# Running sums of the log forget gates: fp32 products replaced by products in the short format, a rounded part and the rest

## The chip, the cores and the metric

The kernel runs on one core of a Trainium2 chip. The metric is the device time of one execution in microseconds (us), lower is better; three timed runs are given for the kernel before, and one further execution was profiled. The core's engines work side by side and meet through semaphores: PE (matrix products; PEld is its loading of the stationary operand), DVE (vector), ACT (activations), POOL (GpSimd) and SP, which here only issues DMAs.

## The reference

A sequence of 256 tokens of width 1024 goes through two blocks. The first has two layers (l = 0, 1), each an RMS norm, a hybrid mixer with three kinds of attention heads (A sparse, B chunk band, C "forgetting"), gates, and a SwiGLU feed-forward. The second block has a MoBA layer and a dilated layer, each with a squared-ReLU feed-forward. The change touches the five C heads of the two layers of the first block:

```python
log_f = jax.nn.log_sigmoid(f_logit.astype(jnp.float32))
F = jnp.moveaxis(jnp.cumsum(log_f, axis=1), 1, 2)
...
logits = (jnp.einsum('bqhd,bshd->bhqs', qs, k).astype(jnp.float32) * scale
          + Fq[..., :, None] - F[:, :, None, :])
```

`F` is the running sum over the 256 tokens of the log of the forget gate, one row for each head; every logit of the head gets the sum at its query minus the sum at its key.

## The kernel before

**Format.** All data is fp32. The large products are made in a short format (`F32R`), in which a number is kept as a rounded part ("hi") and, in a second tile, the rest ("lo"); each product then is hi x hi, lo x hi and hi x lo, three products in place of one. For every unit of weights (two tiles of 128 x 512) a DMA issued by SP fills `raw_units`, ACT rounds it to `hi_units` (L1371), POOL subtracts to get `lo_units` (L733), and PE uses both (L789, L832, L834, L835). Small products, transposes, scores and the sums over the gates are made in plain fp32.

**Tokens.** The 256 tokens are two tiles of 128. P = 128, S = 256, HC = 5 C heads, NT = 2 token tiles.

**Order around the change.** The attention of a layer runs in steps k = 0, 1, 2, ..., one head scored in each, written out by hand on every engine and in order on each. In each step PE transposes (L1013) or scores (L997, L1000) and then works one unit of the gate weights (12 products at L789), so weight products are woven between the heads. In steps 3 to 8 `forget_products` comes in between:

- Step 3 (c = 0): three small products (L1270 to L1272) with the triangular constant `tri` as stationary operand and `LF`, 128 tokens x 5 heads for each token tile, as moving one. They give the running sums with tokens on partitions, and DVE copies them to `F8` (L2188).
- Steps 4 to 8 (c = 1 to 5), one C head each: the head's column of `LF`, broadcast to 128 columns, is the stationary operand, and `tri` is the moving one, 256 columns for the first token tile (L1276) and 256 for the second (L1277). The result is the running sum along the free axis on all 128 partitions of `BANK[TP]`. DVE makes the head's mask of it (`forget_masks`, L2192 and L2193).

`LF` comes from DVE and ACT in the steps before: DVE takes -z and its minimum with z (L2148, L2149, event "nabs"), ACT an exponential (L1715), DVE four small operations (L2154 to L2157), ACT a logarithm (L1718), DVE two more (L2160, L2161, event "logf"), all on 128 x 10 elements. Scratch of this chain (`ZN`, `ZE`, `ZD`) lies in PSUM.

**tri.** It is a 128 x 384 constant: 8 where 128 + p <= column, else 0. Its columns 0 to 127 are all zero, 128 to 255 are the triangle, 256 to 383 are all 8. It lies in the tile `constants`, filled by a DMA.

**POOL.** Beside the `lo_units`, POOL makes eight modulation sums in the first layer (L698, L702), one after every fourth unit from the first gate unit on.

## Time and profile before

| | |
|---|---|
| timed runs | 1460.19, 1459.61, 1456.82 us; median 1459.61 us |
| profiled execution, its own time | 1456.65 us |
| its span (first to last instruction) | 1454.8 us |
| granted TensorE clock, mean | 0.997 |
| PE matrix products | 1432.1 us busy, 98% |
| POOL | 1210.1 us busy, 83% |
| ACT / DVE | 52% / 50% |

The profile lists, for one execution, what each engine did and what released it when it had waited. "Busy" of PE is modelled at its ends, so two products in a row overlap in the records: the duration of one record is more than the time that it takes of the engine. What a product takes of the engine is read from the chain of work that ended last, which divides the time among the instructions one after another. An fp32 product shows as two loads and two matrix records (x2 for one instruction).

### The profile page before, as it was taken

The numbers are of one execution on the slowest core, as the hardware profiler recorded it, in microseconds if no ns is written. First come the engines' busy times: TensorE is split into PE (matmuls) and PEld (weight loads), VectorE is DVE, ScalarE is ACT, GpSimd is POOL, SyncE is SP. The second block draws the span as 40 slices with busy tenths as digits, with TensorE's granted clock in tenths as the row PEclk, the third lists the DMA queues.
The fourth block names the chain that finished last, engine by engine and source line by source line (L and its number), as shares of the span: only waits on it lengthen the run. The fifth ranks groups of instructions, "written<-read, shape, count | busy, mean of one in ns | idle before, by whom it ended". The sixth has DMA issues, their size and how long they took to land.

```text
span 1454.8 us, 21549 instructions
## 1 busy us (share of the span) xinstructions
PE 1432.1 (98%) x7600; PEld 1199.7 (82%) x7600; DVE 723.9 (50%) x1557; ACT 755.6 (52%) x1272; POOL 1210.1 (83%) x984
## 2 busy tenths in 40 slices
PE   7999999999999999999999999999999999999997
PEld 5898777799988987778888888778888888788886
DVE  7863654766643754745566304454650044655202
ACT  4435774644444445765544445674654346655431
POOL 3899989888878986559898997966999977789994
PEclk9999999999999999999999999999999999999999
DMA  9994547689875996337676565644566755456651
GB/s 362 402 354 159 199 168 225 230 292 327 313 265 168 401 319 200 117 99 232 219 242 201 187 204 169 191 142 145 189 195 197 222 162 181 131 164 198 199 197 52
DMA packets 149415, 313.35 MB, mean 215 GB/s; under 512 B 10918, under 2 KB 31802, under 8 KB 149307
## 3 DMA queue, kind: packets, MB, share of 16 engines
q1 hardware_dynamic: 147552, 310.62, 63.8%
q10 hardware_dynamic: 1756, 1.35, 0.3%
q8 instruction: 61, 1.00, 0.3%
q14 instruction: 46, 0.38, 0.1%
HBM read 310.87 MB, written 1.06 MB: 214 GB/s over the span
## 4 chain that ended last, share of the span: by engine, by line
PE 92%; DVE 4%; ACT 1%; POOL 1%; DMA 1%; issue 1%; SPq 0%; DVEq 0%; ACTq 0%
PE bank L789 58%; PE bank L834 12%; PE bank L835 8%; PE bank L832 5%; PE bank L997 1%; PE bank L981 1%; POOL lo_units L733 1%; PE bank L870 1%; PE bank L967 1%; DMA x_rows<-in_x 1%; PE bank L1078 1%; PE bank L1013 1%; PE bank L1049 1%; PE bank L1039 0%; PE bank L1092 0%
## 5 line engine op out<-in xcount | busy, mean ns | idle before, releaser
L733 POOL TENSOR_TENSOR lo_units<-raw_units,hi_units 128x512 fp32r<-128x512 f32 (+3 forms) x928 | 1151.4, 1276 | 221.7 <-ACT hi_units L1371 220.6
L1371 ACT ACTIVATE hi_units<-raw_units 128x1024 fp32r<-128x1024 f32 (+1 forms) x470 | 482.6, 1030 | 411.1 <-PE bank L789 251.9
L789 PE MATMUL bank<-hi_units,turned 128*128 128x512 f32 (+3 forms) x1600 | 441.2, 390 | 1.2 <-DVE turned L1897 0.7
L789 PEld LDWEIGHTS bank<-hi_units,turned 128*128 128x128 f32 x1600 | 291.7, 189 | 53.5 <-issue 3.3
L835 PE MATMUL bank<-turned,lo_units 128*128 128x256 f32 x1024 | 288.0, 281 | 0.0
L789 PE MATMUL bank<-hi_units,turned_wide 128*128 128x512 f32 x992 | 274.5, 391 | 0.0
L834 PE MATMUL bank<-turned,hi_units 128*128 128x512 f32 x736 | 259.2, 397 | 0.0
L789 PE MATMUL bank<-lo_units,turned 128*128 128x512 f32 (+3 forms) x800 | 252.8, 383 | 0.9 <-POOL lo_units L733 0.5
L789 PEld LDWEIGHTS bank<-hi_units,turned_wide 128*128 128x128 f32 x992 | 185.3, 188 | 38.4 <-issue 0.5
L835 PEld LDWEIGHTS bank<-turned,lo_units 128*128 128x128 f32 x1024 | 194.4, 190 | 0.2
L789 PEld LDWEIGHTS bank<-lo_units,turned 128*128 128x128 f32 x800 | 149.7, 188 | 30.6 <-POOL lo_units L733 3.7
L834 PEld LDWEIGHTS bank<-turned,hi_units 128*128 128x128 f32 x736 | 138.1, 188 | 33.1
L789 PE MATMUL bank<-lo_units,turned_wide 128*128 128x512 f32 x496 | 160.8, 390 | 0.0
L1849 DVE SCALAR_TENSOR_TENSOR bank<-ada_units,small,bank 128x512 f32<-128x512 f32 x148 | 111.9, 756 | 31.8 <-DMA ada_units<-in_ada_w 27.0
L789 PEld LDWEIGHTS bank<-lo_units,turned_wide 128*128 128x128 f32 x496 | 93.1, 188 | 20.0 <-POOL lo_units L733 0.4
L1915 DVE TENSOR_REDUCE bank<-bank 128x256 f32<-128x512 f32 x92 | 64.4, 700 | 85.2 <-PE bank L835 84.4
L832 PE MATMUL bank<-turned,hi_units 128*128 128x256 f32 x576 | 104.0, 283 | 0.0
L832 PEld LDWEIGHTS bank<-turned,hi_units 128*128 128x128 f32 x576 | 90.2, 192 | 0.6
L1781 ACT ACTIVATE mlp_relu<-bank 128x256 f32<-128x256 f32 x56 | 21.5, 384 | 59.2 <-DVE bank L1915 58.7
L2321 DVE SCALAR_TENSOR_TENSOR bank<-x_rows,bank 128x512 f32<-128x512 f32 x8 | 5.2, 692 | 87.0 <-PE bank L789 87.0
L1911 DVE TENSOR_TENSOR turned_wide<-bank,turned_wide 128x256 fp32r<-128x256 f32 x92 | 39.0, 424 | 15.9 <-ACT turned_wide L1421 13.2
L2334 DVE SCALAR_TENSOR_TENSOR bank<-x_rows,bank 128x512 f32<-128x512 f32 x8 | 5.6, 696 | 75.8 <-PE bank L789 75.6
(261 smaller groups left out, 1288.6 us busy)
## 6 DMA issues: line engine op xcount, KB each, us to landing
ada_units<-in_ada_w SPq DMA_DIRECT2D x88, 512.0 KB, 7.8
raw_units<-in_w_ffn_tiles SPq DMA_DIRECT2D x72, 512.0 KB, 5.2
raw_units<-in_mlp_w_out SPq DMA_DIRECT2D x64, 512.0 KB, 3.3
raw_units<-in_mlp_w_tiles SPq DMA_DIRECT2D x56, 512.0 KB, 3.2
raw_units<-in_w_in SPq DMA_DIRECT2D x56, 458.0 KB, 9.7
raw_units<-in_w_in SPq DMA_DIRECT2D x48, 512.0 KB, 6.9
raw_units<-in_w_ffn_out SPq DMA_DIRECT2D x44, 512.0 KB, 3.5
raw_units<-in_moba_w_qkv SPq DMA_DIRECT2D x24, 512.0 KB, 3.7
```

Of the source, the lines that this page charges most:

```text
L733: pool.tensor_tensor(LO[:, s, b, 0:w], RAW[:, u["slot"], b, 0:w], HI_[:, s, b, 0:w].bitcast(F32), ALU.subtract).then_inc(lo_ready.sem, lo_ ...
L789: ins = pe.matmul(BANK[2 * c["pair"] + t][:, 0:w], (A[a] if A is BT else A[:, a])[:, part, t * P:(t + 1) * P], W[:, s, b, 0:w], start=(i = ...
L832: pe.matmul(bank[:, 0:S], HI_[:, s, b, at:at + P], A[:, kt, part, :], start=kt == 0 and part == 0, stop=False)
L834: pe.matmul(bank[:, :], HI_[:, s, b, at:at + P], A[:, kt, :, :].rearrange("p two s -> p (two s)"), start=kt == 0, stop=False)
L835: ins = pe.matmul(bank[:, 0:S], LO[:, s, b, at:at + P], A[:, kt, 0, :], start=False, stop=kt == KT - 1)
L870: ins = pe.transpose(BANK[(TQ, TP)[n % 2]][:, j * P:(j + 1) * P], src[:, t, (4 * half + j) * P:(4 * half + j + 1) * P], con("ident"))
L967: pe.matmul(bank[n * DH:(n + 1) * DH, 0:S], src[:, 0, values[n]:values[n] + DH], turned_probs[n][:, 0:S], start=True, stop=False)
L1371: act.activation(HI_[:, s, 0:n, 0:w], RAW[:, u["slot"], 0:n, 0:w], ACT.Copy)\
L1781: act.activation(RTN[:, m % 4, :], BANK[(TQ, TP)[m % 2]][:, 0:S], ACT.Relu).then_inc(act_side.sem, act_side.mark(("relu tile", i, m)))
L1849: ins = v.scalar_tensor_tensor(total, raw[:, k, :], COND[:, kt:kt + 1], partial, ALU.mult, ALU.add)
L1911: tell(v.tensor_tensor(AT[:, n, 1, :], h, AT[:, n, 0, :].bitcast(F32), ALU.subtract), turned_lo, (tag, "tile", n))
L1915: return v.tensor_reduce(to, bank[:, :].rearrange("p (two s) -> p s two", two=2), AX_X, ALU.add)
```

## The change

The products of steps 4 to 8 are made in the short format. DVE writes, once, a rounded copy of the 256 columns of `tri` that are not zero over the constant itself (8 and 0 are the same in the short format). In each layer DVE writes `LF` in two parts into the new tile `forget_rounded`: this turns one operation into four (L2161 before). Each head's two fp32 products become four: rounded part and rest of the first token tile's column against 256 columns of `tri`, and rounded part and rest of the second token tile's against the 128 columns in which the product is not zero. The three products of step 3 stay in fp32, their operand read through a view of the same memory. The new tile is placed after `ones_rounded`, so that the tiles behind it (`raw_units`, `hi_units`, `lo_units` and most others) move up by its 80 bytes, rounded up to 96.

```diff
     ONES = ONES_R[:, :].bitcast(F32)
+    LFR, _ = place("forget_rounded", [P, 2, NT * HC], F32R)
     RAW, _ = place("raw_units", [P, NR, UNIT_K, CW])
...
-    CON, _ = place("constants", [P, n_const])
+    CON, con_at = place("constants", [P, n_const])
+    CON_R, _ = place("constants_rounded", [P, n_const], F32R, at=con_at)
+    TRI_R = CON_R[:, cat["tri"][0] + P:cat["tri"][1]]
+    TRI = TRI_R.bitcast(F32)
...
-                    pe.matmul(BANK[TP][:, 0:HC], con("tri")[:, P:2 * P], lf[:, 0, :], start=True, stop=True)
-                    pe.matmul(BANK[TP][:, HC:2 * HC], con("tri")[:, S:3 * P], lf[:, 0, :], start=True, stop=False)
-                    pe.matmul(BANK[TP][:, HC:2 * HC], con("tri")[:, P:S], lf[:, 1, :], start=False, stop=True)\
+                    pe.matmul(BANK[TP][:, 0:HC], TRI[:, 0:P], lf[:, 0, :], start=True, stop=True)
+                    pe.matmul(BANK[TP][:, HC:2 * HC], TRI[:, P:S], lf[:, 0, :], start=True, stop=False)
+                    pe.matmul(BANK[TP][:, HC:2 * HC], TRI[:, 0:P], lf[:, 1, :], start=False, stop=True)\
                         .then_inc(forget.sem, forget.mark((l, "cols")))
                     return
                 pe.wait_ge(rows.sem, rows.at(("forget cols", l) if c == 1 else ("forget mask", l, c - 2)))
-                pe.matmul(BANK[TP][:, 0:S], LF[:, c - 1:c].to_broadcast([P, P]), con("tri")[:, P:3 * P], start=True, stop=False)
-                pe.matmul(BANK[TP][:, 0:S], LF[:, HC + c - 1:HC + c].to_broadcast([P, P]), con("tri")[:, 0:S], start=False, stop=True)\
-                    .then_inc(forget.sem, forget.mark((l, c - 1)))
+                for t, cols, onto in ((0, slice(0, S), slice(0, S)), (1, slice(0, P), slice(P, S))):
+                    for part in range(2):
+                        ins = pe.matmul(BANK[TP][:, onto], LFR[:, part, t * HC + c - 1:t * HC + c].to_broadcast([P, P]), TRI_R[:, cols],
+                                        start=(t, part) == (0, 0), stop=(t, part) == (1, 1))
+                ins.then_inc(forget.sem, forget.mark((l, c - 1)))
...
             dve.wait_ge(late_const_in, 16)
+            if l == 0:
+                v.tensor_copy(TRI_R, con("tri")[:, P:3 * P])
             z = PROJ[:, :, FC:FC + HC]
...
                     link(v.tensor_tensor(ZL, ZL, ZD, ALU.subtract))
-                    say(v.scalar_tensor_tensor(LF, ZN, 0.0, ZL, ALU.max, ALU.add), ("logf", l))
+                    link(v.scalar_tensor_tensor(ZN, ZN, 0.0, ZL, ALU.max, ALU.add))
+                    v.tensor_copy(LF, ZN)
+                    link(v.tensor_copy(LFR[:, 0, :], ZN))
+                    say(v.tensor_tensor(LFR[:, 1, :], ZN, LFR[:, 0, :].bitcast(F32), ALU.subtract), ("logf", l))
```

`link` makes the next DVE operation wait for this one; `say` raises the event that others wait for.

## Rows read from the trace of the kernel before

**Rows 1.** The page: busy time and share by engine, and the chain by engine.
```profile
PE 1432.1 (98%) x7600; PEld 1199.7 (82%) x7600; DVE 723.9 (50%) x1557; ACT 755.6 (52%) x1272; POOL 1210.1 (83%) x984
...
PE 92%; DVE 4%; ACT 1%; POOL 1%; DMA 1%; issue 1%; SPq 0%; DVEq 0%; ACTq 0%
```

**Rows 2.** Busy time by stretch: us, then each engine, PE clock, DMA share, GB/s.
```profile
125.00:150.00 25.00, 25.00 (x130) 20.10 (x126) 10.59 (x27) 12.42 (x18) 24.31 (x20) 1.00 0.47 154
...
555.00:580.00 25.00, 25.00 (x126) 20.15 (x128) 10.92 (x27) 12.42 (x18) 15.82 (x13) 1.00 0.55 168
```

**Rows 3.** The chain in order of time, 100 to 160 us: start, us, what.
```profile
121.65 0.22 PE bank L1013 x2
...
125.78 0.22 PE bank L1271 x2
...
129.34 0.43 PE bank L1276 x2
129.77 0.43 PE bank L1277 x2
130.21 2.74 PE bank L789 x12
...
133.80 0.63 PE bank L1276 x2
134.43 0.43 PE bank L1277 x2
```

**Rows 4.** Lines L1276 and L1277: min/median/max ns, and who waited (us, times).
```profile
L1276 PEld LDWEIGHTS bank<-constants,small x20: 185/188/193, 129.1 to 575.8; 128*128 128x128 f32 x20
L1276 PE MATMUL bank<-constants,small x20: 379/380/483, 129.2 to 576.1; 128*128 128x256 f32 x20
...
  DVE forget_masks L2192: 25.6, 10
```

**Rows 5.** The chain in order of time, 390 to 430 us, feed-forward of layer 0.
```profile
390.00 0.12 PE bank L835
390.12 0.24 PE bank L832 x2
```

**Rows 6.** The page: one of the costliest groups, loads of a short-format operand.
```profile
L835 PEld LDWEIGHTS bank<-turned,lo_units 128*128 128x128 f32 x1024 | 194.4, 190 | 0.2
```

**Rows 7.** Timeline, 209 to 229 us: start, us, engine, line; [idle before <-releaser].
```profile
209.09 5.02 POOL L733 TENSOR_TENSOR lo_units<-raw_units,hi_units 128x512 fp32r<-128x512 f32 x4
...
217.35 0.38 ACT L1490 ACTIVATE turned<-bank 128x256 fp32r<-128x256 f32 x1 [3.29 <-PE bank L969]
...
218.76 2.54 POOL L733 TENSOR_TENSOR lo_units<-raw_units,hi_units 128x512 fp32r<-128x512 f32 x2 [4.65 <-ACT hi_units L1371]
...
228.67 0.30 PEld L789 LDWEIGHTS bank<-lo_units,mixed_turned 128*128 128x128 f32 x2 [0.30 <-POOL lo_units L733]
```

**Rows 8.** Timeline, 116 to 126 us, the chain that makes LF in layer 0.
```profile
116.56 0.17 DVE L2149 TENSOR_TENSOR small<-bank,proj_rows 128x10 f32<-128x10 f32 x1
...
117.16 0.18 ACT L1715 ACTIVATE bank<-small 128x10 f32<-128x10 f32 x1
...
121.00 0.17 DVE L2161 SCALAR_TENSOR_TENSOR small<-bank,small 128x10 f32<-128x10 f32 x1
...
122.80 0.74 DVE L2029 SCALAR_TENSOR_TENSOR idx_scores<-bank,proj_rows,idx_scores 128x256 f32<-128x256 f32 x2 [1.63 <-ACT bank L1526]
...
125.40 0.39 PE L1270 MATMUL bank<-small,constants 128*128 128x5 f32 x2
```

**Rows 9.** Groups of DVE by shape, 90 to 130 us: busy us, mean ns | idle before.
```profile
L1854 DVE CAST mod_rounded<-bank 128x512 fp32r<-128x512 f32 x1 | 0.7, 691 | 0.0
...
L2133 DVE TENSOR_TENSOR proj_rows<-bank,row_vectors 128x326 f32<-128x326 f32 x2 | 1.0, 488 | 0.0
...
L2133 DVE TENSOR_TENSOR proj_rows<-bank,row_vectors 128x52 f32<-128x52 f32 x2 | 0.4, 202 | 0.0
```

## The prediction, made before the changed kernel ran

> **What bounds the kernel now.** I read the page first: busy shares, then the chain that ended last [rows 1]. PE is busy 98% of the span, and 92% of the chain is PE's. An average can hide a stage with another limit, so the second view is the busy time by stretch over the steps that the change touches: 125 to 150 us in layer 0 and 555 to 580 us in layer 1 [rows 2]. PE is busy in all 25 us of both, at a granted clock of 1.00 (the 2.4 GHz level). DVE and ACT are below half. POOL is not: 24.31 of 25 us in layer 0, 15.82 in layer 1, so in layer 0 a second engine is nearly full, and whether it lets a gain through has to be shown. The third view is the chain in order of time [rows 3]. There PE's instructions follow one another without a foreign piece, and each has its true share of the engine's time. A microsecond less of PE work in these steps is then a microsecond less of the chain, unless something later holds it up.
>
> **The products of one head, before.** The fp32 product of 256 columns takes 0.43 us, the first and the second token tile's alike [rows 3]: 0.86 us a head. In half of the steps the first stands with 0.63 us: there the products of the scores, which use 64 rows, come ahead of it in place of a transpose, and the 0.20 us more is a price of the changeover (a weight product in that place pays about the same), so it stays. The records of one instruction are two, with 188 ns for the load and 380 ns for the product [rows 4]; they overlap, and the 0.43 us is two passes of about 0.216 us. Line L1276 has 20 records, so 10 products: 5 heads in 2 layers, and 10 heads pay 8.6 us in all.
>
> **The products of one head, after.** Two short-format products have 256 columns. The feed-forward of layer 0 has just these: 0.12 us each, 0.24 us for two [rows 5]. That is 256 columns at 2.4 GHz, 0.107 us, and 0.013 us on top. So the first token tile costs 0.24 us.
>
> The second tile's two products have 128 columns, and no short-format product of the trace has so few. Two rows bound them. From below: PE needs a load before each product, and the loads alone set a pace. The small fp32 products of 5 columns take 0.22 us for two passes, 0.11 us a load, and two transposes of 128 columns take 0.22 us, again 0.11 us each [rows 3]. The load's record is as long in the short format (190 ns) as in fp32 (188 ns) [rows 4, 6], so I see no faster load. From above: the fp32 rate, where 256 columns cost 0.43 us, so 128 cost 0.215 us, in case the short format has its speed only at the widths at which this kernel has used it. I take 0.11 us, since the transpose has the same width and the load the same length, and since 256 columns in short format (0.12 us) already are so near the load's pace that a narrower product should meet it. Both ends go into the range.
>
> Sum for a head: 0.24 + 2 x 0.11 = 0.46 us, in place of 0.86 to 0.87 (the chain's 0.43 pieces begin 0.43 and 0.44 us apart, so 0.865). Saved: 0.405 us a head, **4.05 us** for ten. At the upper bound: 0.24 + 0.43 = 0.67, saved 0.195, 1.95 us for ten.
>
> The Trainium skill ("TensorE: Matmul & The Clock Gate", back-to-back issue gap) gives an isolated gap of N/2.4 plus 2.5 ns, 56 ns for 128 columns, and speaks of loads that run during the product before. By that page the two narrow products would cost 0.11 us together and the saving would be about 5 us; the same page's load time, 128 columns at 1.2 GHz or 107 ns, agrees with the 0.11 us of rows 3. It is weighed as a rival below.
>
> **DVE's added work.** In layer 0 one copy of 128 x 256 comes ahead of "nabs". A cast of 128 x 512 took 0.69 us [rows 9], so it costs between 0.2 (the shortest DVE operations) and 0.36 us (half of the cast); I take 0.35. It moves the end of L2149 from 116.73 to about 117.1 us. ACT begins its exponential at 117.16 [rows 8], right behind its own table load, which ended about then: the copy is covered, by less than 0.1 us. Without cover it would cost nothing on PE either, because of the next slack. At "logf" the one operation (0.17 us) is followed by three more, about 0.2 us each with the link: 0.6 us, in each layer. L2161 ends at 121.17 us, and PE comes to L1270 at 125.40 [rows 8]: 4.2 us of slack, 3.6 after the change, 3.2 if the copy's 0.35 us went through. Behind it on DVE waits L2029, at 122.80 after 1.63 us idle, so that 0.6 us fits in too. Layer 1 has the same order and no copy. All of it: 0. If the cover were gone, at most 0.35 + 0.6 + 0.6, about 1.6 us.
>
> **DVE's masks.** L2192 waited 25.6 us over ten heads for L1277 [rows 4]; it will start 0.4 us sooner, and PE does not wait for it. Step 3 keeps its instructions. No DMA is added or moved.
>
> **Does POOL let layer 0's gain through?** From the attention's start POOL works nearly without a pause. But it stops: at 209.09 it does four operations, until 214.11, and is then idle for 4.65 us until ACT's `hi_units`; ACT in turn, in order, had waited 3.29 us for PE's L969 until 217.35 [rows 7]. So at 218.76 POOL is late because PE is, not for its own work. If PE arrives 2.0 us earlier (five heads), so do ACT and POOL, and POOL's pause shrinks to about 2.6 us. After it the one wait of PE for POOL, 0.30 us at 228.67 [rows 7], keeps its size and moves along. I let the whole gain through.
>
> **The sum.** Against the profiled execution: span 1454.8 - 4.05 = 1450.7 us, its own time 1456.65 - 4.05 = 1452.6. That execution lies 3.0 us below the median of the three timed runs, which themselves span 3.4 us. Against the median: 1459.61 - 4.05 = **1455.5 us**, 0.28% less. About 0.3% (4.4 us) is what a measurement of this kernel can tell from no change, so the forecast falls just inside "same".
>
> **Rivals.**
>
> *Narrow short-format products run at the fp32 rate.* For it: nowhere does the kernel use the short format below 256 columns, so no row shows its speed there. Against: nothing in 256, 458 or 512 columns hints at a step. Time 1459.6 - 1.95 = 1457.7 us.
>
> *Narrow products are bound by streaming, not by the load.* For it: loads overlap products in the records. They would cost 0.053 + 0.013 = 0.067 us each; a head 0.37, saved 0.49, in all 4.9 us: 1454.7 us, 0.34% less. Against: transposes and 5-column products at 0.11 us. The Trainium skill's gap (same page) is this rival with another constant.
>
> *Layer 0's gain is lost to POOL.* For it: POOL at 97% in the steps, PE's 0.30 us wait at 228.67. Against: the 4.65 us pause. It decides once PE is ahead by more than the pause. If all of layer 0 were lost, 2.0 us are left: 1457.6 us; with narrow products at the fp32 rate, 1.0 us: 1458.6 us.
>
> *Slower: the 96-byte move of the tiles.* Nearly all big tiles start at another address. If POOL's subtraction (2.51 us for a unit, two of its five-microsecond four) were slower at the new address, it would reach PE's 2.74 us a unit [rows 3, 7] at 9% more. From there every per cent costs 0.025 us on some 460 units, 11.5 us; one per cent over the point would end at about 1467 us. Against: DVE's additions at L2133 start at columns of all sorts, yet 52 and 326 columns took 202 and 488 ns [rows 9], 1.04 ns a column, with other widths on the same line: engines don't mind the address there.
>
> **Chances.** Forecast (load-bound) 0.42; fp32 rate 0.32; streaming-bound 0.08; layer 0 lost, wholly or partly 0.10; slower by the move or by something unforeseen 0.08. Range: from the streaming case, 1454.7, less half the spread of the runs (1.7), 1453.0, to the lost case with the fp32 rate, 1458.6, plus 1.2 for the spread of a median, 1459.8. It leaves out the slower case and little else. Faster by over 0.3% (below 1455.2): forecast 0.42 x 0.4, streaming 0.08 x 0.8, fp32 rate 0.32 x 0.05: 0.25. Slower: 0.08. Same: 0.67.
>
> **What would show it.** In the chain of the changed kernel each head's four products should take 0.12, 0.12, 0.11 and 0.11 us; 0.21 in the last two is the fp32 rate, 0.07 is streaming. They should have one record each, not two, with loads of about 188 ns. The small operations before "logf" should end near 121.8 us with PE's L1270 unmoved at 125.4. POOL's pause near 218 us should be about 2.6 us and PE's wait at 228 us still 0.3. The step from 129 to 147 us in layer 0 should be 2.0 us shorter, and every later landmark earlier by the same amount up to layer 1, then by 4.0. The prediction is wrong if the products cost more than 0.86 us a head, if PE waits for `lo_units` or `hi_units` where it did not, or if POOL's 1.25 us an operation has changed.

## The result, and the profile after

The change made the kernel slower by 0.3%: 1462.95 us, the median of 7 runs (1460.90 to 1464.31), against 1459.13 us for the kernel before in 7 runs beside them; ratio 1.0029, 95% interval 1.0018 to 1.0041. The forecast was 1455.5 us, and its range (1453.0 to 1459.8) does not hold the result. The profiled execution has a span of 1462.1 us, 7.3 more than before's. That is more than the medians' 3.8 us, since before's profiled execution lies 2.5 us below its median and the changed kernel's 1.0 above: what is read from this pair of traces is exact for the two executions and larger than the loss of a typical one.

The page of the changed kernel, busy time and chain, answers to [rows 1]:

```profile
PE 1431.4 (98%) x7600; PEld 1194.6 (82%) x7600; DVE 724.0 (50%) x1564; ACT 755.6 (52%) x1272; POOL 1209.6 (83%) x984
...
PE 70%; DMA 11%; POOL 9%; DVE 6%; ACT 3%; issue 1%; SPq 1%; DVEq 0%; ACTq 0%; POOLq 0%
...
L737 POOL TENSOR_TENSOR lo_units<-raw_units,hi_units 128x512 fp32r<-128x512 f32 (+3 forms) x928 | 1150.8, 1276 | 229.5 <-ACT hi_units L1377 227.9
```

The busy times are those of before, POOL's 1276 ns for one operation too. What changed is who holds the chain: DMA 11% and POOL 9%, in place of 1% each. (Lines behind the new code stand four to eleven further down: L793 is the old L789, L1001 the old L997, L1377 the old L1371, L1282 the new products.) PE's waits, us in total, times, longest:

```profile
PE bank L1001 <- DVE idx_scores L2035: 4.0, 1, 4.0
PE bank L793 <- ACT hi_units L1377: 2.6, 3, 1.1
PE bank L1001 <- ACT qk_turned L1521: 1.4, 1, 1.4
```

Before had one wait of 0.5 us for `hi_units`, ahead of the changed steps, and neither of the other two. The busy table of the steps answers to [rows 2]; layer 0's stretch has 4 us less of PE, with 136 GB/s moved in it:

```profile
125.00:150.00 25.00, 20.99 (x107) 16.80 (x104) 8.14 (x21) 10.46 (x15) 24.31 (x19) 0.93 0.43 136
555.00:580.00 25.00, 25.00 (x137) 19.91 (x138) 10.36 (x32) 16.18 (x24) 21.49 (x18) 1.00 0.79 256
```

The granted clock of layer 0's stretch is 0.93 too, where before had 1.00. That is taken up after the wait.

The chain through the 4.0 us wait, in order of time (answers to [rows 3]):

```profile
132.55 6.48 DMA raw_units<-in_w_in
...
139.05 0.03 ACT hi_units L1377
...
140.13 1.28 ACT L1715
...
141.43 1.06 ACT gate_rows L1715
142.48 0.27 ACT qk_turned L1521
...
143.27 0.75 DVE idx_scores L2035 x2
...
144.15 0.70 PE bank L1001 x4
...
146.05 4.04 PE bank L793 x12
```

DVE is named as the releaser, but it only passes on a delay that came with a transfer. Raw units landed at 139.03 us; ACT works in order, so the table load, the gates and the scores' inputs queued behind its `hi_units`. The timelines of ACT, first before, then after:

```profile
135.12 1.06 ACT L1371 ACTIVATE hi_units<-raw_units 128x1024 fp32r<-128x1024 f32 x1 [0.81 <-DMA raw_units<-in_w_in]
```

```profile
139.05 1.06 ACT L1377 ACTIVATE hi_units<-raw_units 128x1024 fp32r<-128x1024 f32 x1 [5.34 <-DMA raw_units<-in_w_in]
```

ACT was already waiting 0.81 us for this transfer before, and now the transfer lands 3.9 us later. PE still had about 0.9 us of slack behind it: DVE ended its part at 140.3 us, and PE came to those scores at 141.36. After the change DVE ends 3.7 us later and PE comes 1.2 us sooner (140.14 us); less the slack, that makes the 4.0 us.

Of the 3.9 us only 1.7 are the transfer's own time (6.48 us in place of 4.82). For 2.3 us it was issued later, and it was issued later because POOL, which frees the raw units, was later. First the issue by SP, before and after (two issues to a row), then POOL, before and after:

```profile
130.28 0.98 SPq L675 DMA_DIRECT2D raw_units<-in_w_in  x2
```

```profile
132.55 1.80 SPq L679 DMA_DIRECT2D raw_units<-in_w_in  x2
```

```profile
83.95 25.24 POOL L733 TENSOR_TENSOR lo_units<-raw_units,hi_units 128x458 fp32r<-128x458 f32 x22
```

```profile
91.62 7.03 POOL L737 TENSOR_TENSOR lo_units<-raw_units,hi_units 128x458 fp32r<-128x458 f32 x6 [0.82 <-ACT hi_units L1377]
98.89 6.81 POOL L737 TENSOR_TENSOR lo_units<-raw_units,hi_units 128x456 fp32r<-128x456 f32 x6 [0.25 <-ACT hi_units L1377]
106.67 4.81 POOL L737 TENSOR_TENSOR lo_units<-raw_units,hi_units 128x456 fp32r<-128x456 f32 x4 [0.97 <-ACT hi_units L1377]
```

Before, POOL worked from 84 to 109 us without a pause. Now it ran out of input three times, 2.0 us in all, and each time ACT's rounding ahead of it had waited for a transfer. From 106.67 us to beyond 180 us POOL is full in both kernels, so it stays 2.3 us late and the transfers that wait for it with it.

The wait has a second price. Right behind it the granted clock fell to the 1.2 GHz level, from 145.1 to 148.5 us: the mean of this stretch is 0.52 (1.00 before), PE's products stand 427 ns apart, and one unit takes 4.04 us in place of 2.74. Against the products-alone kernel below, without this wait, PE lost 1.6 us there:

```profile
145.00:148.50 3.50, 3.50 (x12) 2.93 (x11) 1.48 (x4) 1.44 (x2) 3.24 (x4) 0.52 0.00 0
```

And the transfers themselves are slower. Busy by stretch, in a stretch where the DMA engines are full (last two numbers: DMA share, GB/s), before, then after:

```profile
18.00:44.00 26.00, 23.86 (x125) 19.11 (x124) 21.16 (x34) 12.11 (x18) 14.22 (x12) 0.93 1.05 403
```

```profile
18.00:44.00 26.00, 23.94 (x125) 19.09 (x124) 20.32 (x34) 12.22 (x18) 13.38 (x12) 0.93 1.05 368
```

The DMA share is the same 1.05, the bytes are 9% fewer. The change adds no transfer. It moves where they land: `raw_units` from byte 38528 to 38624 of each partition, the tiles of the adaLN rows from 122496 and 151808 to 122592 and 151904. (From `mod_rows` on the tiles move by 128 bytes, since that tile is placed on the next multiple of 64.)

To compare kernels, the rest of this text divides the time between two landmarks, the start of PE's instruction 500 (at 115.8 us, ahead of all changed products) and its last one, into PE's waits and the time without them, called pace. Before: 1330.4 us, 5.1 of it waits. All such figures are of one execution a kernel.

| kernel | total, us more | waits | products | other pace |
|---|---|---|---|---|
| the change | +7.65 | +7.9 | -4.0 | +3.8 |

The -4.0 is measured below; the last column is what is left, and the fallen clock is 1.6 us of it. So the products gave what was forecast, and the move of the tiles took more, in three ways: waits for late transfers, the clock behind the longest of them, and a PE that runs slower without waiting. In this pair of traces it took nearly three times as much (11.7 us), by the medians of the next section 6.8 us.

### The profile page after: what moved, and what is told of

Read it like the earlier page. It is cut to its first block, busy times and chain, and to the rows that moved or that the text cites. A ratio compares the mean times of both kernels' runs of the same rounds, so it can differ in the third digit from the quotient of the medians.

```text
span 1462.1 us, 21556 instructions
## 1 busy us (share of the span) xinstructions
PE 1431.4 (98%) x7600; PEld 1194.6 (82%) x7600; DVE 724.0 (50%) x1564; ACT 755.6 (52%) x1272; POOL 1209.6 (83%) x984
## 3 DMA queue, kind: packets, MB, share of 16 engines
q10 hardware_dynamic: 1756, 1.35, 0.3%
## 4 chain that ended last, share of the span: by engine, by line
PE 70%; DMA 11%; POOL 9%; DVE 6%; ACT 3%; issue 1%; SPq 1%; DVEq 0%; ACTq 0%; POOLq 0%
PE bank L793 44%; PE bank L838 12%; POOL lo_units L737 8%; PE bank L839 6%; DMA raw_units<-in_w_in 4%; DMA raw_units<-in_w_ffn_tiles 3%; DMA ada_units<-in_ada_w 2%; ACT hi_units L1377 1%; DVE bank L1855 1%; DMA raw_units<-in_w_ffn_out 1%; PE bank L1001 1%; PE bank L985 1%; PE bank L874 1%; PE bank L971 1%; DMA x_rows<-in_x 1%
## 5 line engine op out<-in xcount | busy, mean ns | idle before, releaser
L737 POOL TENSOR_TENSOR lo_units<-raw_units,hi_units 128x512 fp32r<-128x512 f32 (+3 forms) x928 | 1150.8, 1276 | 229.5 <-ACT hi_units L1377 227.9
L1377 ACT ACTIVATE hi_units<-raw_units 128x1024 fp32r<-128x1024 f32 (+1 forms) x470 | 482.9, 1031 | 422.3 <-PE bank L793 210.0
L793 PE MATMUL bank<-hi_units,turned 128*128 128x512 f32 (+3 forms) x1600 | 444.2, 392 | 2.3 <-ACT hi_units L1377 1.7
L793 PEld LDWEIGHTS bank<-hi_units,turned 128*128 128x128 f32 x1600 | 291.4, 189 | 58.0 <-issue 3.3
L793 PE MATMUL bank<-hi_units,turned_wide 128*128 128x512 f32 x992 | 274.7, 391 | 0.9 <-ACT hi_units L1377 0.9
L793 PE MATMUL bank<-lo_units,turned 128*128 128x512 f32 (+3 forms) x800 | 255.2, 386 | 1.0 <-POOL lo_units L737 0.6
L838 PE MATMUL bank<-turned,hi_units 128*128 128x512 f32 x736 | 255.8, 392 | 0.0
L793 PEld LDWEIGHTS bank<-hi_units,turned_wide 128*128 128x128 f32 x992 | 185.2, 188 | 39.8 <-issue 1.8
L793 PEld LDWEIGHTS bank<-lo_units,turned 128*128 128x128 f32 x800 | 149.8, 188 | 33.0 <-POOL lo_units L737 4.3
L793 PE MATMUL bank<-lo_units,turned_wide 128*128 128x512 f32 x496 | 161.0, 390 | 0.6 <-POOL lo_units L737 0.5
L793 PEld LDWEIGHTS bank<-lo_units,turned_wide 128*128 128x128 f32 x496 | 93.0, 188 | 21.3 <-POOL lo_units L737 1.9
```

Of the source, the lines that this page charges most:

```text
L737: pool.tensor_tensor(LO[:, s, b, 0:w], RAW[:, u["slot"], b, 0:w], HI_[:, s, b, 0:w].bitcast(F32), ALU.subtract).then_inc(lo_ready.sem, lo_ ...
L793: ins = pe.matmul(BANK[2 * c["pair"] + t][:, 0:w], (A[a] if A is BT else A[:, a])[:, part, t * P:(t + 1) * P], W[:, s, b, 0:w], start=(i = ...
L838: pe.matmul(bank[:, :], HI_[:, s, b, at:at + P], A[:, kt, :, :].rearrange("p two s -> p (two s)"), start=kt == 0, stop=False)
L1377: act.activation(HI_[:, s, 0:n, 0:w], RAW[:, u["slot"], 0:n, 0:w], ACT.Copy)\
```

## The experiments

**Move and products apart.** The first kernel is the one before with a gap of 96 bytes; the second is the change with `forget_rounded` placed last, so that no tile moves.

```diff
     ONES = ONES_R[:, :].bitcast(F32)
+    plan_at[0] += 96
     RAW, _ = place("raw_units", [P, NR, UNIT_K, CW])
```

> The kernel before, with nothing changed but an empty gap of 96 bytes ahead of raw_units, so that raw_units, hi_units, lo_units and the tiles behind move as they do in the changed kernel. Theory A (the move slows the DMAs: from 17 us on each 512 KB transfer of the changed kernel landed 1.36 us after the one before it, against 1.25 before): transfers of the first 100 us at about 1.36 us, the attention of layer 0 stalls PE for some 4 us near 144 us, and the time is 1459 + 4 (what the products save, now missing) + 3.8 = about 1466 to 1468 us, ratio 1.005 or more. Theory B (the added DVE work or the order of the products made the stalls, the slower DMAs are chance): 1.25 us a transfer, no stall at 144 us, ratio 1.000.

```diff
-    LFR, _ = place("forget_rounded", [P, 2, NT * HC], F32R)
     RAW, _ = place("raw_units", [P, NR, UNIT_K, CW])
...
     POS, _ = place("positions_int", [P, NT], I32)
+    LFR, _ = place("forget_rounded", [P, 2, NT * HC], F32R)
```

> The changed kernel, with forget_rounded placed behind the last tile, so that every tile of the kernel before stays at its address. Theory A: no stall near 144 us, transfers at 1.25 us, four products of a head at 0.41 us, ratio 0.997 (1459.1 - 4.4 = 1454.7 us). Theory B: the stall of 4 us stays, ratio 1.003.

The gap alone: 1465.90 us, ratio 1.0045 (1.0033 to 1.0057). The products alone: 1455.48 us, ratio 0.9979 (0.9970 to 0.9987). That this is the forecast to 0.02 us is luck: by its ratio it is 3.1 us less than before, by the medians of that round (1459.12 before) 3.6, and 4.05 were forecast. The same stretch as above, of the gap and then of the products:

```profile
18.00:44.00 26.00, 25.68 (x118) 20.72 (x117) 20.45 (x33) 10.89 (x17) 12.91 (x11) 0.93 1.05 368
```

```profile
18.00:44.00 26.00, 25.91 (x119) 20.91 (x118) 20.44 (x33) 11.07 (x17) 12.66 (x11) 0.93 1.05 403
```

The gap alone slows the transfers as the change did. Its wait near 144 us was 1.1 us, not the 4 that I expected, and its clock did not fall there: PE comes to the same late data at 142.7 us in place of 140.1, about half of it by its longer products and half because instruction 500 started 1.3 us later in this execution. From instruction 500 to 700 the second kernel gains 2.0 us, over layer 1's heads (3000 to 3300) 2.0 again: 4.0 us, with `LFR` and all else of the change in place. It doesn't keep all of it. A wait of PE at 180.6 us grew from 0.27 to 0.82 us, and the chain leads back from there over DVE, ACT and a transfer to POOL, which holds 11% of this kernel's chain.

**Other distances of the move.** The change with 32 more bytes behind `forget_rounded` (all moves by 128) or 160 more (by 256), and the kernel before with a gap of 64 or 32.

```diff
     LFR, _ = place("forget_rounded", [P, 2, NT * HC], F32R)
+    plan_at[0] += 32     # after128; 160: after256
```

> The changed kernel, with 32 bytes of padding behind forget_rounded, so that the tiles move by 128 bytes in place of 96. If it is the address within 64 bytes (theory A1), transfers at 1.25 us and ratio 0.997, as without a move. If any move from the addresses of the kernel before slows (A2, neighbours or wider alignment), 1.36 us and 1.003. Theory B: 1.003.

> The changed kernel with 160 bytes of padding behind forget_rounded, so that the tiles move by 256 bytes and lie in the 256-byte windows as in the kernel before. Theory G: as with forget_rounded placed last: ada_units 1.25 us and raw_units 1.18 us a transfer, ratio 0.998, 1455.5 us. If it is the distance moved or the neighbours in memory that counts: 1458 us or more, as with 128 bytes.

```diff
+    plan_at[0] += 64     # hole64; 32: hole32
     RAW, _ = place("raw_units", [P, NR, UNIT_K, CW])
```

> The kernel before with an empty gap of 64 bytes ahead of raw_units. A1 (64 bytes are the grain): 1.25 us a transfer, ratio 1.000. If the grain is 128 bytes (A3): slower transfers, ratio 1.005. Theory B: ratio 1.000.

> The kernel before with an empty gap of 32 bytes ahead of raw_units. Theory G (a row of a transfer costs by the number of 256-byte windows of the destination that it touches): raw_units then starts 160 bytes into a window, its rows of 1832 bytes (160 + 1832 = 1992) touch 8 windows as before (128 + 1832 = 1960), and go at about 77 ns a packet; rows of 2048 bytes touch 9 unless they start on a window. So it behaves like the gap of 64 bytes: transfers of raw_units at 1.2 us, of ada_units at 1.36, ratio 1.000 to 1.002. Theory H (a start that is no multiple of 64 bytes is slow): as the gap of 96 bytes: 88 ns a packet, 1.34 us, ratio 1.0045.

Measured: moved by 128, 1458.65 us, ratio 1.0007 (0.9990 to 1.0023); its profiled execution took 1465.32 us, far above that median, so its waits are not used here. Moved by 256, 1456.45, ratio 0.9981 (0.9963 to 0.9999): the gain is back. Gap of 64, 1459.59, 1.0006 (0.9993 to 1.0019). Gap of 32, 1464.28, 1.0042 (1.0028 to 1.0057). The last is a miss that points ahead: its packets of 1832 bytes took 78 ns, as the window theory has it, and yet it is as slow as the 96-byte gap.

The time between two landings in a full stretch, from the traces, gives the rule. A unit of full rows (2048 bytes each) into the adaLN tiles takes 1.25 to 1.27 us where the tile starts on a multiple of 256 and 1.35 to 1.36 us where it doesn't; the packets of 1832 bytes into `raw_units` take 76 to 78 ns each (median) with the tile at 0, 128, 160 or 192 modulo 256, and 88 ns at 224 (the change and the 96-byte gap). Counted in windows of 256 bytes, 2048 bytes touch 8 on a multiple and 9 elsewhere; 1832 bytes touch 8 from any of the first four places and 9 from 224. The Trainium skill ("DMA: Bandwidth & Descriptors", section "How a descriptor splits into AXI transactions") gives the split into 256-byte transactions as the vendor's account, and words its rule for an unaligned start as one of reading; these rows show the like on the side that is written, in the core's memory. A ninth window is 12.5% more; 8% (1.35 against 1.25 us) and 14% (1.34 against 1.18 us for a raw unit) were measured.

**All bulk destinations on multiples of 256.** The products-alone kernel, and the kernel before, with the plan's start, `gate_rows`, `mod_rows` and `scores` rounded up.

```diff
-    plan_at = [-(-nc.sbuf_base // 64) * 64]
+    plan_at = [-(-nc.sbuf_base // 256) * 256]
...
     PROJ, union = place("proj_rows", [P, NT, PROJ_W])
+    plan_at[0] = -(-plan_at[0] // 256) * 256
...
-    MOD, mod_at = place("mod_rows", [P, 6 * D], at=-(-one_end // 64) * 64)
+    MOD, mod_at = place("mod_rows", [P, 6 * D], at=-(-one_end // 256) * 256)
```

> The changed kernel with forget_rounded last and every tile that a DMA fills starting on a multiple of 256 bytes (all tiles 128 bytes up, gate_rows and mod_rows padded to the next multiple). Theory G: the last transfers of 9 windows a row go too: the first units of ada_units from 1.35 to 1.25 us each, and raw_units with 2048-byte rows. PE waits for these only in the first 60 us, so 0.5 to 2 us less than with forget_rounded last alone: 1453.5 to 1455 us, ratio 0.996 to 0.9975. Without G: no difference from 0.998.

> The kernel before with all tiles that a DMA fills on multiples of 256 bytes, as in the aligned changed kernel. If placement and products add up: 1458.95 - (1455.5 - 1452.0) = 1455.5 us, ratio 0.9977, and the aligned changed kernel is 4 us below it. If the alignment only paid together with shorter products: ratio 1.000.

With the change's products 1451.99 us, ratio 0.9956 (0.9940 to 0.9971), the fastest kernel of all; without them 1455.19, ratio 0.9981 (0.9966 to 0.9997). Difference 3.2 us (by the two ratios 3.6): products and placement add up. But the full stretch is not faster than before's 403:

```profile
18.00:44.00 26.00, 24.32 (x123) 19.80 (x122) 20.23 (x32) 11.06 (x16) 13.50 (x12) 0.93 1.05 402
```

**Which products pay.** The products-alone kernel with the second token tile on 256 columns, as the first; and the kernel before, still fp32, with only the second token tile narrowed to 128.

```diff
-                for t, cols, onto in ((0, slice(0, S), slice(0, S)), (1, slice(0, P), slice(P, S))):
+                for t, cols in ((0, slice(P, 3 * P)), (1, slice(0, S))):
```

> forget_rounded last, and the second token tile's two products on 256 columns, the first 128 against the zeros of tri, as in the kernel before (the rounded copy is made of 384 columns). It measures what the narrow products save. Load-bound narrow products (0.11 us): 0.02 us a head, ratio as with narrow ones, 0.998. Streaming-bound (0.06 us, as their starts in the trace of the changed kernel lie apart): 0.12 us a head, 1.2 us in all, ratio 0.9987.

```diff
-                pe.matmul(BANK[TP][:, 0:S], LF[:, HC + c - 1:HC + c].to_broadcast([P, P]), con("tri")[:, 0:S], start=False, stop=True)\
+                pe.matmul(BANK[TP][:, P:S], LF[:, HC + c - 1:HC + c].to_broadcast([P, P]), con("tri")[:, P:S], start=False, stop=True)\
```

> The kernel before with one edit: the fp32 product of the second token tile on its 128 columns that are not zero. It needs no rounding, no tile and no DVE work. 128 columns at the fp32 pace are 0.215 us, so 0.215 us a head are saved, 2.15 us in all: 1456.8 us, ratio 0.9985. If a narrow fp32 product were held to the wide one's time: 1.000.

The full width takes 1455.95 us, ratio 0.9978 (0.9963 to 0.9992), no different from 1455.48. The fp32 kernel takes 1456.86, ratio 0.9985 (0.9968 to 1.0003), which as a time is not clear of no change; between the landmarks its two groups of heads take 1.0 us less each. A head in the chain, in order of time, narrow short format (products alone), full short format, narrow fp32:

```profile
558.89 0.40 PE bank L1282 x4
559.29 2.81 PE bank L793 x12
```

```profile
558.56 0.47 PE bank L1283 x4
559.02 2.75 PE bank L794 x12
```

```profile
129.63 0.43 PE bank L1276 x2
130.06 0.22 PE bank L1277 x2
130.28 2.73 PE bank L789 x12
```

The narrow products save 0.07 us, and the weight products behind them take 0.06 to 0.07 us longer: 3.21 and 3.22 us. In the short format the narrowing is worth nothing; in fp32 it halves the second product.

**Transfers or something else?** Two kernels split the gap: 96 bytes ahead of `raw_units` with 160 more ahead of `proj_rows`, and 64 bytes ahead of `proj_rows` alone.

```diff
+    plan_at[0] += 96     # rawonly
     RAW, _ = place("raw_units", [P, NR, UNIT_K, CW])
...
+    plan_at[0] += 160    # rawonly; 64 here and nothing above: adaonly
     PROJ, union = place("proj_rows", [P, NT, PROJ_W])
```

> The kernel before with a gap of 96 bytes ahead of raw_units and one of 160 ahead of proj_rows: raw_units, hi_units, lo_units and row_vectors lie as in the changed kernel, the tiles behind as in the kernel before within their 256-byte windows. Transfers of raw_units at 88 ns a packet and 1.33 us, of ada_units at 1.25. If the windows of raw_units make the loss of the changed kernel: stalls of PE near 144 or 420 us and ratio 1.003 or more. If it is those of ada_units: ratio 1.000.

> The kernel before with a gap of 64 bytes ahead of proj_rows: raw_units, hi_units and lo_units stay, ada_units loses its place on a multiple of 256. Transfers of raw_units at 76 ns a packet and 1.18 us, of ada_units at 1.35 us. As with the gap of 64 bytes ahead of raw_units: ratio 1.000 to 1.001 if ada_units alone costs nothing. If it carries the loss: 1.003.

They took 1466.65 us (1.0053, 1.0033 to 1.0073) and 1464.99 us (1.0044, 1.0028 to 1.0059). These are the slow branches of both expectations, but without the stalls that were to make them: between the landmarks their waits are 0.2 and 0.3 us shorter than before's. All of the loss, 9.9 and 6.3 us, is pace. The theory that only late transfers cost time falls. In the last 90 us PE does nothing but 512-column products on `hi_units` or `lo_units` and `turned_wide`; the busy table there, before, then the 64-byte kernel:

```profile
1380.00:1440.00 60.00, 60.00 (x266) 49.67 (x266) 2.59 (x4) 21.29 (x21) 53.21 (x42) 1.00 0.42 140
```

```profile
1380.00:1440.00 60.00, 60.00 (x259) 48.32 (x258) 2.59 (x4) 22.51 (x22) 54.79 (x44) 1.00 0.49 158
```

259 products in place of 266 in 60 us, at a granted clock of 1.00 and with no wait. The transfers there are far from full (0.49). Sorted by operands, these products start 233 ns apart in place of 227, while those on `turned` keep their 227; in the kernels with one gap it is the other way round. What `turned_wide` and `turned` share is the second operand, so the next theory was the distance between the two operands, modulo 256 bytes, which is 0 for both pairs before.

**Operand distance alone.** Three edits of the kernel before, each with 256 bytes in two parts, so that at most one thing changes modulo 256: `turned` (distance), `hi_units` with `lo_units` (distance to both), `raw_units` (a destination, no distance).

```diff
+    plan_at[0] += 96     # turned96
     HT, turned_at = place("turned", [P, KT, 2, S], F32R)
...
+    plan_at[0] += 160    # turned96; 96: raw96
     RAW, _ = place("raw_units", [P, NR, UNIT_K, CW])
+    plan_at[0] += 96     # hi96; 160: raw96
     HI_, _ = place("hi_units", [P, NH, UNIT_K, CW], F32R)
     LO, _ = place("lo_units", [P, NH, UNIT_K, CW], F32R)
+    plan_at[0] += 160    # hi96
     VEC, _ = place("row_vectors", [P, NV, CW])
```

> The kernel before with only turned (and the small tiles behind it) moved by 96 bytes, all others by 256: DMA destinations keep their place modulo 256, the distance from turned to hi_units changes by 160 modulo 256. Distance theory: products on hi_units and turned start 231 ns apart in place of 227, those on turned_wide stay at 227; feed-forward of layer 0 a little faster; no new waits; DMA 403 GB/s; in all 2 to 4 us more: about 1462 us. Rival (PE's pace follows the slower transfers): pace and time as before, 1459 us.

> The kernel before with 96 bytes between raw_units and hi_units and 160 behind lo_units: no bulk DMA destination changes modulo 256, hi_units and lo_units move against both turned and turned_wide. Distance theory: products on turned and on turned_wide both start 231 to 233 ns apart, as in the run that moved the raw units by 96 and the rest by 256; DMA 403 GB/s, no new waits; 7 to 10 us more: 1466 to 1469 us. Rival (slower transfers set PE's pace): 1459 us.

> The kernel before with 96 bytes ahead of raw_units and 160 behind it, so that only raw_units stand at another place modulo 256 (224 in place of 128). Window theory for the transfers: rows of 1832 bytes touch 9 windows of 256 in place of 8, DMA falls to about 384 GB/s in 18 to 44 us. Distance theory: PE's pace is untouched (227 ns with either operand). What is left are waits for late raw units, near none where only raw units are slow: 1459 to 1461 us. Rival (the earlier run's 7.5 us came from the raw units' place): 1466 us.

All three came out as the distance theory has it in the main: 1462.78 us (1.0029, 1.0014 to 1.0044), 1468.06 us (1.0065, 1.0043 to 1.0088) and 1457.79 us (0.9993, 0.9980 to 1.0006). The first missed in its details: products on `turned` start 234 ns apart and not 231, and layer 0's feed-forward was not faster (107.5 us, before 107.4). The full stretch of the second and third:

```profile
18.00:44.00 26.00, 24.32 (x123) 19.81 (x122) 20.20 (x32) 11.07 (x17) 13.50 (x12) 0.93 1.05 403
```

```profile
18.00:44.00 26.00, 25.32 (x118) 19.91 (x117) 20.38 (x32) 10.54 (x16) 11.99 (x11) 0.80 1.05 386
```

The slowest kernel of all has transfers as fast as before's; the one with slower transfers loses nothing that can be measured. The last 90 us, of `turned96` and of `hi96`:

```profile
1380.00:1440.00 60.00, 60.00 (x266) 49.69 (x265) 2.59 (x4) 23.32 (x22) 56.12 (x45) 1.00 0.51 167
```

```profile
1380.00:1440.00 60.00, 60.00 (x259) 48.27 (x258) 2.59 (x4) 23.08 (x22) 54.46 (x44) 1.00 0.50 166
```

Only the kernel in which `turned_wide`'s distance changed is slow here.

**Can distance be used for a gain?** In the kernel with the 64-byte gap layer 0's feed-forward (256-column products on `turned`) ran faster, 114 ns a product in place of 120. The aligned kernel with `turned` moved by 64, or by 192, and the rest by 256:

```diff
+    plan_at[0] += 64     # turned64; 192: turned192
     HT, turned_at = place("turned", [P, KT, 2, S], F32R)
...
+    plan_at[0] += 192    # turned64; 64: turned192
     RAW, _ = place("raw_units", [P, NR, UNIT_K, CW])
```

> The aligned kernel with the tile turned moved by 64 bytes and everything behind it by 256, so that only the distance from turned to hi_units and lo_units is changed against 256-byte multiples (it was whole) and every tile that DMA fills in bulk stays on a multiple of 256. Distance theory (PE's pace depends on how far apart its two operands lie, modulo 256 bytes): the 768 products of 256 columns in layer 0's feed-forward start 114 ns apart in place of 120, 4.2 us less; the 512-column products with turned gain or lose under 1 us; time 1452.0 - 4.2 = 1447.8 us, DMA at 402 GB/s in 18 to 44 us. Rival (the pace in the 64-byte kernel came from slower DMA writes, not from the distance): 1452.0 us and 120 ns.

> The aligned kernel with turned moved by 192 bytes and everything behind it by 256, so that hi_units lie 64 bytes further from turned, modulo 256, as in the kernel of before with a 64-byte gap (the run that moved turned by 64 had them 64 bytes nearer, the other sign, and its feed-forward products started 118 ns apart). Distance theory with its sign: layer 0's feed-forward products on turned and hi_units start 114 ns apart (120 when the distance is whole), 4.2 us less in 304 to 404 us; the products of 512 columns with turned 2 ns more at the median, those with turned_wide 227; the 64-byte run's pace without its waits was 1.5 us ahead of before from 116 us on, which gives 1452.0 - 1.5 = 1450.5 us. Rival (that pace belonged to the places of other tiles, or to the slower transfers, in the 64-byte run): 118 or 120 ns, 1452 us or more.

1460.13 us (1.0021, 1.0005 to 1.0037) and 1456.23 us (0.9986, 0.9977 to 0.9996); both missed their times. The 256-column products start 118 ns apart in the first and 116 in the mean in the second, where the 864 of them in layer 0 took 103.8 us in place of 107.4. With the same distance of 64 the gap kernel had 113 at the median, so the distance alone does not set this number. And the second kernel's other stretches were 5.9 us slower than the aligned kernel's, and its waits 1.2 us longer. My sum had taken the 64-byte kernel's 1.5 us off the aligned kernel, whose pace was already 2.4 us ahead of before. The aligned kernel with whole distances stays the best.

The parts between the two landmarks against before, in us (the pace of kernels with the change's products has their -4.0 in it), and the median time between the starts of two products that follow each other on these operands, in ns. The columns of 512 are the products that stream the weights (L789), the last one is layer 0's feed-forward:

| kernel | hi_units minus turned, mod 256 | hi_units minus turned_wide | waits | pace | 512 columns, turned | 512, turned_wide | 256, turned |
|---|---|---|---|---|---|---|---|
| before | 0 | 0 | 0 | 0 | 227 | 227 | 120 |
| products alone | 0 | 0 | +1.0 | -2.8 | 227 | 227 | 120 |
| the change, moved by 256 | 0 | 0 | +0.6 | -5.3 | 228 | 227 | 120 |
| aligned | 0 | 0 | +0.8 | -6.4 | 228 | 227 | 120 |
| before, aligned | 0 | 0 | +0.3 | -2.3 | 227 | 227 | 120 |
| the change | 96 | 0 | +7.9 | -0.2 | 232 | 227 | 117 |
| the change, moved by 128 | 128 | 0 | +2.1 | +0.5 | 232 | 227 | 119 |
| gap 96 | 96 | 0 | +3.8 | +2.9 | 232 | 227 | 117 |
| gap 64 | 64 | 0 | +4.3 | -1.5 | 229 | 227 | 113 |
| aligned, turned by 64 | 192 | 0 | +0.6 | +1.2 | 233 | 227 | 118 |
| aligned, turned by 192 | 64 | 0 | +2.0 | -4.2 | 229 | 227 | 117 |
| gap 32 | 32 | 0 | +0.8 | +6.0 | 234 | 227 | 117 |
| 64 ahead of proj_rows | 0 | 192 | -0.3 | +6.3 | 227 | 233 | 120 |
| 96 and 160 | 96 | 96 | -0.2 | +9.9 | 232 | 232 | 118 |
| turned by 96 | 160 | 0 | +0.8 | +6.4 | 234 | 227 | 119 |
| hi_units by 96 | 96 | 96 | -0.9 | +9.9 | 232 | 232 | 118 |
| raw_units by 96 | 0 | 0 | +0.2 | +0.2 | 227 | 227 | 120 |

The rule holds for one shape of product. Where the weights are loaded and `turned` is streamed, the 256-column products are slowest at 0 (120 ns, elsewhere 113 to 119), and the 512-column ones (L834) follow no rule that I can read: 230 to 236 ns at distance 0, 230 to 235 elsewhere.

## Why the prediction was wrong

**What bounds the kernel.** Right, but read in one place only. PE holds the chain, and the steps of [rows 2] had no wait on it. I did not look at what feeds the steps: ACT waited 0.81 us for a transfer at 135.12 us, with the table load, the gates and the scores' inputs in order behind it, and PE's slack there was about 0.9 us.

**The products.** Right in sum and in both layers: 4.0 us measured, 4.05 forecast. Its parts were not: the narrow products start 0.06 us apart, the streaming rival's number, and not 0.11. In the chain a head's four take 0.40 us where 0.46 were forecast, and the weight products behind give the difference back. From starts in the trace of the change (the four begin at 128.84, 129.04, 129.16 and 129.22 us, the next product at 129.33), four narrow and wide ones together take 0.49 us:

```profile
128.84 0.66 PE L1282 MATMUL bank<-constants_rounded,forget_rounded 128*128 128x256 f32 x4
129.33 0.69 PE L793 MATMUL bank<-hi_units,turned 128*128 128x512 f32 x2
```

So the sum came out right by luck: what the narrow ones save over 0.11 us is lost at the change to wide products.

**DVE.** Right. The copy took 0.30 us, and the operations before "logf" ended at 121.3 us (forecast 121.8), with PE's step 3 at its place, 0.3 us earlier than before:

```profile
115.96 0.30 DVE L2153 CAST constants_rounded<-constants 128x256 fp32r<-128x256 f32 x1
...
121.14 0.17 DVE L2172 TENSOR_TENSOR forget_rounded<-bank,forget_rounded 128x10 fp32r<-128x10 f32 x1
```

**"I let the whole gain through."** This step failed too, in part. In the changed kernel POOL's pause before 222.82 us is 4.74 us, and not the 2.6 that I forecast, because PE came late and not early. Where PE does come early (products alone), the pause is 3.35 us, POOL holds 11% of the chain, and PE's wait at 180.6 us takes back 0.55 of layer 0's 2.0 us: the rival "lost to POOL" was real, and small. In the changed kernel POOL did not become slower (1276 ns as before), but at 24.31 of 25 us it could not catch up the 2.3 us for which it had lacked input, and so it passed them on to the transfers and to PE. The change and the 96-byte gap differ by the products alone, and their medians by 3.0 us. In their two traces nothing of the 4.0 us is left: the wait near 144 us is 4.0 in place of 1.1, and only behind the long one did the clock fall.

**"No DMA is added or moved", and "engines don't mind the address there".** These are the steps that failed. The first counted instructions and not destinations: all bulk destinations moved, by 96 or 128 bytes, and the rows of `raw_units` and of the adaLN tiles that had stood on a multiple of 256 then crossed nine windows of 256 bytes in place of eight. The second took DVE's additions for all engines. They do not mind, and neither does POOL (1276 ns as before), but PE does: 227 ns became 232 as soon as its two operands stood 96 bytes further apart modulo 256. The rival that I named for the slow side had the right cause, the 96-byte move, but priced it only through POOL's speed, found it no slower, and gave it 0.08 together with everything unforeseen. The sum has no term for either effect; both stood at nothing.

**What stays open.** Why PE's pace follows the operands' distance was not found; the runs show that it does, for two pairs of tiles and with the transfers left alone. Two steps, at 977 to 1129 and 1286 to 1357 us, each take 1.3 us more or less in kernels with equal distances. The kernel with the narrow fp32 product, which moves no tile, shows both (+1.3 and -1.3), and the products concerned are those that load the weights (L834). So a pace in the table is uncertain by about 1.3 us, and the 1.3 us that the aligned kernel gained there is not shown to come from its alignment; no run tells by what these steps change. The waits of the changed kernel were not tested with its distances kept (moving the whole plan by 96 bytes, operands and destinations alike, would do that); that the slower transfers cause them rests on the issues and landings in the chain and on the kernels with fast transfers, which lack the waits at 144 and 555 us (two of them, `turned` by 96 and by 192, have 0.6 and 0.7 us for `hi_units` near 420 us, where the change had 0.9). How long the wait at 144 us is in a typical execution of the changed kernel, and whether the clock falls in it, is not known: one execution was profiled. With `raw_units` alone at 224 no wait came, and their packets took 81 to 84 ns in 18 to 44 us, not 88 (a unit 1.27 to 1.32 us, 384 to 386 GB/s): the count of windows gives the direction, and not this half-way size.

## What to carry to other kernels

A small tile added in the middle of a plan is an edit of every tile behind it: put it at the end, or round it up to the grid that the others stand on. Keep tiles that DMA fills in bulk on multiples of 256 bytes. Try the two operands of the products that stream the weights a multiple of 256 bytes apart: that was best here for 512 columns, and not for the other kinds. And before a gain on the bounding engine is let through, look for waits on transfers that are already above zero on the engines that feed it, and follow such a transfer back to what lets it be issued: a full engine there cannot make up for time once lost.

## What the runs showed of the hardware

- The place of a destination changes a transfer's speed: 403 GB/s in a full stretch, 368 with 9 windows of 256 bytes touched in place of 8; 76 and 88 ns for a packet of 1832 bytes. The DMA share read 1.05 in both.
- PE's 512-column short-format products that stream the weights start 227 or 228 ns apart when its operands' tiles are a multiple of 256 bytes apart and 229 to 234 ns at distances of 32 to 192. 256-column ones that load them: 120 ns at 0, 113 and 117 at 64, 117 to 119 at the other distances.
- Behind a wait of PE of 4.0 us the granted clock fell to the 1.2 GHz level from 145.1 to 148.5 us, at a cost of 1.6 us; behind one of 1.1 us in the same place it did not.
- Short-format products of 128 columns start 0.06 us apart, so no load of 0.11 us holds them back; the 512-column product that follows is later by what they saved.
- A second fp32 product on half its columns saved 0.21 us, half its 0.43.
